# Block products in another order: the second sum last in its pair, the fourth third in the next pair, and the small projection's input loaded one pair earlier

## The reference

```python
y = (...) @ w_out                                    # 512 x 2048 by 2048 x 2048
x = _layernorm(DEEPNORM_ALPHA * x + y, post_ln_g[i], post_ln_b[i])
x = x + (p[i] @ ple_w[i]) * jax.nn.sigmoid(x @ ple_gate_w[i])
```

## Time and profile before

| what | value |
|---|---|
| median of 3 runs | 2092.15 us (2092.03 to 2092.24) |
| profiled execution, its own time | 2093.16 us |
| its span, first to last instruction | 2091.5 us |
| PE busy | 2081.2 us, 100% of the span |
| DVE busy | 1341.1 us, 64% |
| ACT busy | 873.3 us, 42% |
| POOL busy | 394.8 us, 19% |
| folded and last pairs of layer 0, layer 1 | about 861 to 986 us, 1758 to 1883 us |

### The profile page before, as it was taken

One profiled execution on the slowest core, in us unless ns is written; L12 is line 12 of the kernel. 1 busy time (PEld: TensorE's weight loads), 2 busy tenths in 40 slices (PEclk: granted clock), 3 DMA queues, 4 the chain that ended last, 5 costly groups with the idle time before them and its releaser, 6 DMA issues.

```text
span 2091.5 us, 29899 instructions
## 1 busy us (share of the span) xinstructions
PE 2081.2 (100%) x11050; PEld 1750.7 (84%) x11050; DVE 1341.1 (64%) x2295; ACT 873.3 (42%) x1148; POOL 394.8 (19%) x232
## 2 busy tenths in 40 slices
PE   9999999999999999999999999999999999999999
PEld 7878888888888888898788888888888888997888
DVE  5235575665765747787733588888888986887332
ACT  4225464464564657354622322222223453447221
POOL 0000000000000004110400034444857521104000
PEclk9999999999999999999999999999999999999999
DMA  8322222212222122684333322222222235852431
GB/s 320 141 101 88 75 80 80 78 63 81 71 90 80 60 80 81 167 221 145 106 109 121 136 100 85 96 101 101 98 87 98 101 121 128 214 159 81 144 110 69
DMA packets 46947, 233.51 MB, mean 112 GB/s; under 512 B 5456, under 2 KB 5728, under 8 KB 26896
## 3 DMA queue, kind: packets, MB, share of 16 engines
q1 hardware_dynamic: 35424, 190.33, 26.4%
q0 software_dynamic: 10000, 36.36, 7.0%
q10 hardware_dynamic: 1440, 5.77, 0.8%
HBM read 224.05 MB, written 8.39 MB: 111 GB/s over the span
## 4 chain that ended last, share of the span: by engine, by line
PE 97%; DMA 1%; ACT 1%; DVE 1%; issue 0%; ACTq 0%
PE G L745 84%; PE X L745 8%; PE T L745 5%; DMA w_raw<-wall_in 1%; PE T L927 1%; PE T L1048 0%; ACT w_hi L1484 0%; DVE w_lo L2194 0%; ACT a_hi L1235 0%; ACT Z L1430 0%; ACT Y L1577 0%; PE T L1053 0%; PE T L899 0%; DVE Y L2222 0%; ACT L1322 0%
## 5 line engine op out<-in xcount | busy, mean ns | idle before, releaser
L745 PE MATMUL G<-a_hi,w_hi 128*128 128x512 f32 (+1 forms) x2524 | 979.9, 388 | 3.3 <-DVE w_lo L2194 2.8
L745 PE MATMUL G<-a_hi,w_lo 128*128 128x512 f32 (+1 forms) x2524 | 974.0, 386 | 0.0
L745 PE MATMUL G<-a_lo,w_hi 128*128 128x512 f32 (+1 forms) x2524 | 972.2, 386 | 0.0
L1231 ACT ACTIVATE w_hi<-w_raw 128x2048 fp32r<-128x2048 f32 x147 | 281.7, 1916 | 788.0 <-PE G L745 775.2
L1705 DVE TENSOR_TENSOR w_lo<-w_raw,w_hi 128x2048 fp32r<-128x2048 f32 x104 | 242.1, 2328 | 494.7 <-ACT w_hi L1231 494.7
L745 PEld LDWEIGHTS G<-a_hi,w_hi 128*128 128x128 f32 x2524 | 474.2, 188 | 101.2 <-issue 4.0
L745 PEld LDWEIGHTS G<-a_hi,w_lo 128*128 128x128 f32 x2524 | 474.2, 188 | 95.7 <-issue 0.2
L745 PEld LDWEIGHTS G<-a_lo,w_hi 128*128 128x128 f32 x2524 | 474.3, 188 | 95.0 <-issue 0.5
L2429 DVE SCALAR_TENSOR_TENSOR T<-tmp,par,T 128x512 f32<-128x512 f32 x464 | 306.9, 749 | 0.0
L687 POOL TENSOR_TENSOR w_lo<-w_raw,w_hi 128x2048 fp32r<-128x2048 f32 x45 | 207.8, 4617 | 232.4 <-ACT w_hi L1231 232.4
L1484 ACT ACTIVATE w_hi<-w_raw 128x768 fp32r<-128x768 f32 (+1 forms) x86 | 66.3, 784 | 90.5 <-PE G L745 30.4
(11 more groups left out here) (336 smaller groups left out, 2249.2 us busy)
## 6 DMA issues: line engine op xcount, KB each, us to landing
w_raw<-wall_in SPq DMA_DIRECT2D x150, 1024.0 KB, 4.8
w_raw<-wall_in SPq DMA_DIRECT2D x42, 384.0 KB, 4.9
w_raw<-wall_in SPq DMA_DIRECT2D x36, 256.0 KB, 5.0
w_raw<-wall_in POOLq DMA_DIRECT2D x24, 384.0 KB, 5.4
Y<-w_in POOLq DMA_DIRECT2D x2, 2048.0 KB, 15.5
x_residual<-Y POOLq DMA_DIRECT2D x16, 256.0 KB, 3.6
out<-Y POOLq DMA_DIRECT2D x15, 256.0 KB, 3.6
Z<-xT_in SPq DMA_DIRECT2D x6, 512.0 KB, 9.2
```

The costliest lines, as they stand in the source:

```text
L745: return pe.matmul(o, l, r, start=start, stop=stop)
L1231: f(w_hi[:, w.slot, :], w_raw[:, w.slot, :], ACT.Copy).then_inc(S("w_hi"), 1)
```

## The change

- In all folded pairs the product of t2 is the last of its pair, behind b22 and b21, and the product of t4 is made in the next pair, behind r1 and r2 (in pair 7 too). High parts, low parts and the ring follow that order. In pair 7 the slots of b12 and b22 change places.
- POOL's list stays, so the sum for t4 and the two sums for the next pair are issued when the low part of t2 is done, which is later in the pair now. SP's list stays too: b21 of pair 3 still waits for the low part of pair 2's t4, and b12 of pair 7 for that of pair 6's t4, which are now made in pairs 3 and 7.
- `empty_products` is cut in two: `empty_most` (four operations) right after the low part of t2, `empty_rest` (three operations, behind t2's product) after the low part of t4 in the next pair.
- DVE's queue in pairs 3 to 6 is now: r1, r2, t4 of the pair before, `empty_rest`, finish_two, b11, t1, finish_one, `full_add`, t3, `full_add`, the bank copy, (pair 4 of layer 0: the small projection's input), centres, (a square), b22, b21, a square, t2, `empty_most`, a square.
- ACT issues the transfer of a pair's residual at the end of the pair before.
- POOL issues the small projection's input at the end of pair 2's list, and ACT rounds it at the end of pair 3.

```diff
-FOLDED = ("r1", "r2", "b11", "t1", "t3", "t2", "b22", "b21", "t4")
-FIRST_FOLDED = ("r1", "t1", "r2", "b11", "t3", "t2", "b22", "b21", "t4")
+FOLDED = ("r1", "r2", "b11", "t1", "t3", "b22", "b21", "t2")
+FIRST_FOLDED = ("r1", "t1", "r2", "b11", "t3", "b22", "b21", "t2")
...
-UNFOLDED_SLOTS = {"b12": 3, "b22": 2}
+UNFOLDED_SLOTS = {"b12": 2, "b22": 3}
...
+SEQUENCE = pieces(FOLD_FROM)
+for pair in range(FOLD_FROM + 1, FOLD_TO + 1):
+    SEQUENCE += pieces(pair)[:2] + [(pair - 1, "t4")] + pieces(pair)[2:]
+N_PIECES = len(SEQUENCE)
...
@@ POOL, weight_sums @@
-                    if (layer, p) == (0, FOLD_FROM + 1):
+                    if (layer, p) == (0, FOLD_FROM):
...
@@ PE, folded_pair @@
                 if p > FOLD_FROM:
+                    last_product(layer, p - 1)
                     pe.wait_ge(*emptied(layer, p - 1, 6))
...
+                piece_products(layer, p, "b22", two[:, 0:HALF_T], *fold(3), False, True).then_inc(done, 1)
+                piece_products(layer, p, "b21", one[:, 0:HALF_T], *tokens(twos_at, 0), False, False).then_inc(done, 1)
                 pe.wait_ge(*emptied(layer, p, 1))
                 piece_products(layer, p, "t2", first, *fold(2), True, True).then_inc(done, 1)
-                piece_products(layer, p, "b22", two[:, 0:HALF_T], *fold(3), False, True).then_inc(done, 1)
-                piece_products(layer, p, "b21", one[:, 0:HALF_T], *tokens(twos_at, 0), False, False).then_inc(done, 1)
-                piece_products(layer, p, "t4", one[:, HALF_T:T], *tokens(twos_at, 1), False, True).then_inc(done, 1)
...
@@ ACT, pairs 3 to 6 @@
                     piece_high(p, "r1")
                     piece_high(p, "r2")
+                    piece_high(p - 1, "t4")
+                    piece_high(p, "b11")
                     act.wait_ge(*summed(layer, p, "t1"))
                     act.wait_ge(*low_made(layer, p - 1, "b21" if p == FOLD_FROM + 1 else "t4"))
                     f(later, chain, ACT.Copy).then_inc(S("base_copied"), 1)
-                    piece_high(p, "b11")
...
                     piece_high(p, "b21")
-                    for n in c[-2:]:
-                        out_square(n)
-                    piece_high(p, "t4")
+                    out_square(c[-2])
+                    piece_high(p, "t2")
+                    if p + 1 < FOLD_TO:
+                        load_residual(p + 1)
+                    out_square(c[-1])
+                    if (layer, p) == (0, FOLD_FROM + 1):
+                        act.wait_ge(S("p_landed"), 16)
+                        f(p_hi.rearrange("p k t -> p (k t)"), p_raw0, ACT.Copy).then_inc(S("p_hi"), 1)
...
@@ DVE, pairs 3 to 6 @@
-                    lows(p, "r1")
+                    lows(p, "r1", "r2")
+                    lows(p - 1, "t4")
+                    empty_rest(p - 1)
                     finish_two(p - 1)
-                    lows(p, "r2", "b11")
+                    residual_in(p)
+                    lows(p, "b11", "t1")
                     finish_one(p - 1)
                     full_add(2 * p - 2)
-                    lows(p, "t1")
+                    lows(p, "t3")
                     full_add(2 * p - 1)
-                    lows(p, "t3", "t2")
                     empty_first(p)
...
-                    lows(p, "b22")
-                    lows(p, "b21")
+                    lows(p, "b22", "b21")
                     square_sums(c[-2:-1])
-                    lows(p, "t4")
+                    lows(p, "t2")
+                    empty_most(p)
                     square_sums(c[-1:])
-                    residual_in(p)
-                    empty_products(p)
```

More of the change, by code:

```diff
@@ L92, with pieces @@
 N_FOLDS = FOLD_TO - FOLD_FROM
-N_PIECES = N_FOLDS * len(FOLDED) + len(UNFOLDED)
+def pieces(p):
+    own = UNFOLDED if p == FOLD_TO else FIRST_FOLDED if p == FOLD_FROM else FOLDED
+    return [(p, name) for name in own]
+SEQUENCE = pieces(FOLD_FROM)
+for pair in range(FOLD_FROM + 1, FOLD_TO + 1):
+    SEQUENCE += pieces(pair)[:2] + [(pair - 1, "t4")] + pieces(pair)[2:]
+N_PIECES = len(SEQUENCE)
 HALVES = (64, 32, 16, 8)
@@ L460, in ring_free @@
             if (p, name) == (FOLD_TO, "b12"):
+                return piece_done(layer, p - 1, "t4")
+            if (p, name) == (FOLD_TO, "b22"):
                 return piece_done(layer, p, "b11")
@@ L1110, in piece_products, with tokens, last_product @@
                 return last
+            def tokens(chunks, half):
+                at = slice(half * HALF_T, (half + 1) * HALF_T)
+                return [a_hi[:, c, at] for c in chunks], [a_lo[:, c, at] for c in chunks]
+            def last_product(layer, p):
+                one, twos_at = out_banks(p)[0], range(PLAIN_K + PAIR_K, KC)
+                piece_products(layer, p, "t4", one[:, HALF_T:T], *tokens(twos_at, 1), False, True).then_inc(S("piece_done"), 1)
             def folded_pair(layer, p):
@@ L1545, in second_part @@
                     piece_high(p, "b21")
[L1546 to L1550 removed]
+                    out_square(c[-2])
+                    piece_high(p, "t2")
+                    if p + 1 < FOLD_TO:
+                        load_residual(p + 1)
+                    out_square(c[-1])
+                    if (layer, p) == (0, FOLD_FROM + 1):
+                        act.wait_ge(S("p_landed"), 16)
+                        f(p_hi.rearrange("p k t -> p (k t)"), p_raw0, ACT.Copy).then_inc(S("p_hi"), 1)
+                piece_high(FOLD_TO, "r1")
+                piece_high(FOLD_TO, "r2")
+                piece_high(FOLD_TO - 1, "t4")
+                piece_high(FOLD_TO, "b11")
+                piece_high(FOLD_TO, "b21")
                 out_square(11)
@@ L2217, in empty_products, with empty_rest @@
                     tt(Y4[:, two, 1, :], Y4[:, two, 1, :], q7, ALU.subtract).then_inc(step, 1)
+                def empty_rest(p):
+                    one, two = 2 * p, 2 * p + 1
+                    q6, step = TB[0][:, 0:HALF_T], S("fold_emptied")
+                    dve.wait_ge(*emptied(layer, p, 5))
                     dve.wait_ge(*piece_done(layer, p, "t2"))
```

41 lines of the change are left out of this document (16 added, 25 removed).

## The result

The changed kernel takes 2098.88 us (median of 8 runs, 2097.72 to 2101.26) beside 2092.54 (2092.03 to 2094.32) for the kernel before on the same chip: ratio 1.0031, 95% interval 1.0022 to 1.0039. It is slower by 6.3 us, which is more than the 0.2% that a measurement of this kernel can tell. The profiled execution took 2099.08, 5.9 more than the profiled one before. In the code of after, the matmuls are L754, the low parts L2216, the high parts L1499, finish_one is L2263, the copy of the next pair's base L1508, and the copy of t1's sum L1551.

The account below looks back on a forecast made before the run. PE was taken to bound the kernel, busy 2081.2 of 2091.5 us, with at most 5.6 us of waits to win. Terms -2.6 + 1.0 + 3.5 = +1.9 us on the median 2092.15 gave 2094.0, range 2090.3 to 2098.0.

Parts of the forecast that it names:

- the start of finish_one in pairs 4 to 6: DVE, pairs 4 to 6: finish_one waits for t4's product and starts 0.20 to 0.25 us after PE's end.
- Pair 2: First folded pair: waits at t4 and r1 go, b21 still waits behind ACT's copy; gain 2.6 us (bounds -0.2 and 5.6).
- SP's load "at nothing": SP's load of pair 3's b21 waits for t4's low part, with r1, r2, b11 of pair 4 behind: no cost.
- its own 2.63: Pair 2, both layers: 2.63 us from the start of ACT's copy to b21's first matmul.
- b22 of pair 3, +1.0: Pair 3: b22 can start at S + 18.8, PE there at S + 18.5; +1.0 us (bounds 0 and 9.6).
- The other steps at nothing: Residual's earlier transfer, b12's load in the last pair, the small projection's input and its split on ACT: no cost.
- DVE's tail: Pairs 4 to 6: DVE work from finish_one to the end of b22's low part, 6.51 us against PE's 6.48.
- The forecast's gap: Before b22, pairs 4 to 6: 0.40 us lost each, 1.54 in layer 0's pair 4; sum +3.5 us (bounds 0, 5.0).
- A: POOL's queue becomes late: three sums back to back, t3's late, each b22 0.69 later in 8 pairs; 2099.5 us; chance 0.22.
- B: No relief: pair 3's b11 lands as before, +2.8 us on the forecast, 2096.8 us; chance 0.12.
- D: DVE's tail doesn't reach PE in pairs 4 to 6: -2.6 + 1.0, 2090.5 us; chance 0.09.
- C: Equal turns between DMA queues: relief is whole, pair 2 has no gap; -1.1 us, 2091.0 us; chance 0.07.

Follow-up runs that it names:

- the two orders: Each alone against the changed kernel: b21's high part ahead of ACT's copy, 2095.70 us; b22's low part ahead of small projection's input and centres on DVE, 2095.10 us.
- both orders: Changed kernel with b21's high part ahead of ACT's copy and b22's low part ahead of the centres on DVE: 2092.63 us, ratio 1.0002 to before.
- the best version: t4's move alone against the kernel before, transfers in their old places, pair 3's r1 low part ahead of the emptying: 2088.87 us, ratio 0.9985.

## Why the prediction was wrong

It said 2094.0, from 2090.3 to 2098.0, most likely no change; it is 2098.88, and slower. The losses after were put at 7.5 us and were 11.2: 0.8 less in pair 2, 1.8 more in pair 3, 2.7 more in pairs 4 to 6. Two steps failed, the one at nothing that makes pair 3's wait, and the start of finish_one in pairs 4 to 6.

**Pair 2: right in its mechanism, a little better than said.** The waits for t4's sum and at r1 went, and b21 waits behind the copy. ACT's timeline of after, the copies and the two uses of sums, beside the earlier trace rows:

```profile
874.23 0.85 ACT L1508 ACTIVATE chain<-w_raw 128x768 f32<-128x768 f32 x1 [7.09 <-DMA w_raw<-wall_in]
...
896.26 0.84 ACT L1508 ACTIVATE chain<-w_raw 128x768 f32<-128x768 f32 x1 [6.27 <-DMA w_raw<-wall_in]
...
905.85 1.58 ACT L1499 ACTIVATE w_hi<-w_raw 128x768 fp32r<-128x768 f32 x2 [4.25 <-DMA w_raw<-wall_in]
909.40 0.85 ACT L1551 ACTIVATE w_raw<-chain 128x768 f32<-128x768 f32 x1 [1.96 <-DMA chain<-wall_in]
...
1774.52 0.85 ACT L1508 ACTIVATE chain<-w_raw 128x768 f32<-128x768 f32 x1 [6.35 <-DMA w_raw<-wall_in]
...
1796.09 0.84 ACT L1508 ACTIVATE chain<-w_raw 128x768 f32<-128x768 f32 x1 [5.80 <-DMA w_raw<-wall_in]
...
1810.06 0.84 ACT L1551 ACTIVATE w_raw<-chain 128x768 f32<-128x768 f32 x1 [3.53 <-DMA chain<-wall_in]
```

From each copy to b21's first matmul it is 2.63 us, in all four places, as in the earlier trace rows. Against before, with the later start of the stretch taken off (0.45 and 4.56), b11 of pair 3 landed 0.97 earlier in layer 0 (forecast 1.18) and 2.53 in layer 1 (forecast 1.59). The gain was 5.8 - 2.2 = 3.6 where 2.6 was said.

**The first step that failed: SP's load "at nothing".** The prediction saw the queue (b21 of pair 3 waits for t4's low part, and r1, r2 and b11 of pair 4 stand behind it) and the time at which b11 is wanted, some 10 us after t4's low part. It set no time of issue and landing beside that. By its own 2.63, b21 of pair 3 (due at 898.89 - 1.36 = 897.53) needs the copy at 894.90, which is 10.0 after SP's first issue behind t4's low part (884.91): the 10 us were right. The chain of waits in after shows when b11 was asked for and came:

```profile
878.58 4.44 DMA w_raw<-wall_in
883.05 0.86 ACT w_hi L1499
...
887.10 0.97 DVE w_lo L2216
888.09 8.10 DMA w_raw<-wall_in
...
```

It was issued at 888.09, when the low part of pair 3's b11 was done, and landed 8.1 us later, 11.3 after SP's issue at 884.91. PE doesn't stand in this chain from 875 to 925. 6.8 us would have done. A term of 1.36 + 0.89 and its slow steps was missing. The one in its place (b22 of pair 3, +1.0) was not there: it came from a t4's sum of 5.78 us, and the sum took 4.4. In layer 0 of the run with SP's other order, r1 and r2 no longer wait for t4's low part, b11 is issued at about the same time (888.19), and its copy starts at 894.58, 1.7 sooner. So part of the 8.1 is due to the loads that this wait held back until just ahead of b11. What else lay there? The DMA queues from 884 to 896.3 us, in after and then in before:

```profile
q0 software_dynamic: 482, 1.42, 50.7%
q1 hardware_dynamic: 731, 1.74, 40.5%
```

```profile
q1 hardware_dynamic: 577, 1.31, 34.9%
q0 software_dynamic: 279, 0.78, 34.3%
q10 hardware_dynamic: 144, 0.79, 16.7%
```

The residual (q10) has left this stretch, as the change wants, but two sums and the small projection's input have entered it. The engines are busy for 91% of it, before for 86%. Moving the input back alone changed nothing, and moving the residual back made the copy 2.2 later. How much of the 8.1 is each neighbour's stays open. The other steps at nothing held: no piece of the last pair starts late, nor does the small input's rounding stop PE.

**The second step that failed, in pairs 4 to 6: when finish_one starts.** DVE's tail behind it was sized right. The forecast's gap, 0.30 and in layer 0's pair 4 1.14 more, assumes that finish_one starts 0.20 after t4's end. DVE's timeline of after, pair 4 of layer 0:

```profile
911.01 0.96 DVE L2216 TENSOR_TENSOR w_lo<-chain,w_hi 128x768 fp32r<-128x768 f32 x1
911.88 0.68 DVE L2263 TENSOR_TENSOR Y<-Y,G 128x512 f32<-128x512 f32 x1
```

b11 began at 911.08, so finish_one should have stood at 911.28; it starts at 911.88. Two sums made it late. t4's came at 905.85, and from t4's low part on DVE has no pause up to b11's low part at 909.91; behind that, t1's low part (0.88) and the step to finish_one (0.86) would have given 911.65, 0.37 late. t1's sum added the other 0.23. The lateness of finish_one (its start less b11's start less 0.20) explains each gap:

| b22 of | finish_one late | late sum | gap due: 0.30 + that (+ 1.14) | gap measured |
|---|---|---|---|---|
| pair 4, layer 0 | 0.60 | t4's 0.37, t1's 0.23 | 2.04 | 2.01 |
| pair 5, layer 0 | 0.23 | t4's | 0.53 | 0.81 |
| pair 6, layer 0 | 0 | none | 0.30 | 0.26 |
| pair 4, layer 1 | 1.44 | t1's | 1.74 | 1.70 |
| pair 5, layer 1 | 0 | none | 0.30 | 0.27 |
| pair 6, layer 1 | 0.30 | t4's | 0.60 | 0.55 |

(In pair 5 of layer 0 DVE also idles 0.22 before t3's low part.) In pair 5 of layer 0 and in pair 6 of layer 1 DVE doesn't idle before t1's low part; it idles before t4's, and all behind that is as much later. Pair 5 of layer 0, DVE's timeline, then ACT's:

```profile
929.26 0.96 DVE L2216 TENSOR_TENSOR w_lo<-w_raw,w_hi 128x768 fp32r<-128x768 f32 x1 [3.90 <-ACT w_hi L1499]
```

```profile
928.38 1.58 ACT L1499 ACTIVATE w_hi<-w_raw 128x768 fp32r<-128x768 f32 x2 [5.68 <-DMA w_raw<-wall_in]
```

So DVE's tail was sized to a few hundredths, and the 2.7 us beyond the forecast's 3.5 come from late sums: 1.7 from t1's in two places, 0.9 from t4's in three. The prediction followed the landing of t4's sum only into pair 3, and its sum had nothing for t1's.

**The rivals.** A comes nearest in time (2099.5), and half of its mechanism is real: sums issued in a row after t2 come late. But the late ones are t1's and t4's, not t3's; together they cost 2.6 us in four places, not 0.69 in each of eight, and t3's low part kept DVE idle once only, for 0.22. B fell (b11 of pair 3 came earlier), D fell (b22 was late in every pair). C fell too. Its rule was that of the Trainium skill, DMA: Bandwidth & Descriptors, section Queues, rings and completion order: a DMA engine takes turns between the queues that have work. The shares of 50.7% and 40.5% above are near to equal turns. Those of the earlier trace rows are not, and POOL's queue was not short of work there: t4's sum was under way from 867.97 for 10.07 us, and beside its 16.8% SP's queue had 79.4%, in layer 1 73.6% beside 21.2%. So no run bears out equal shares as a rule. Nor did POOL's share bound the relief, which in layer 1 was 2.53 against the 1.59 of POOL's time.

**In sum.** t2 last takes the cover of b21 away and makes three sums begin late; undoing it alone gives 6.3 us back. About half of that shows through ACT's copy and half through DVE's tail (3.2 and 3.8 by the two orders). t4's move doesn't need t2's, and is worth 3.4 us with r1's low part brought forward, if the transfers stay where they were; as the change made it, with the early transfers, it was worth nothing (2092.63).

**Still open.** Why landings scatter. For the same code, b21 of pair 2 lost 1.49 in layer 0 and 0.75 in layer 1, and in the run with SP's order 1.8 in both. The 3.6 us between the median with both orders and 2089 are open too. Which neighbour held which transfer can't be settled from single profiles.

## What to carry to other kernels

A step that is set at nothing because "it is asked for early enough" needs two times beside each other, when it is wanted and when its transfer lands under the load that the change itself puts there; here that was 8.1 us for 384 KB, where 6.8 would have done. Try the parts of a change alone: here t4's move gained 3.4 us once its transfers were put back, and t2's move lost 6.3. Moving a load within a stretch where the DMA engines are 90% busy moves the late landing, and by layer 1's profiles its price changed sign with the order of the pieces around it. Follow every late transfer through the in-order queues behind it: in pair 5 of layer 0 a t4's sum that landed late, at 928.38, showed only at b22, at 941.04. And look at the granted clock behind a long wait of PE.

## What the hardware did that was not expected

**The third sum waits for the first to land.** POOL issues t4's, t1's and t3's sums in this order, and nothing in the program holds the third once its base has landed. POOL's timeline of after, pair 4:

```profile
900.77 0.86 POOL L638 DMA_DIRECT2D w_raw<-wall_in  x1 [13.20 <-DVE w_lo L2216]
901.31 1.21 POOL L635 DMA_DIRECT2D chain<-wall_in  x1
906.09 0.88 POOL L635 DMA_DIRECT2D other<-wall_in  x1 [3.57 <-issue]
```

The third goes out at 906.09, 0.24 after t4's sum had landed (905.85); in the other three pairs of layer 0 it is 0.33, 0.34 and 0.34. Before it was the same, t4's landing at 897.52 and then:

```profile
897.76 0.89 POOL L626 DMA_DIRECT2D other<-wall_in  x1 [3.16 <-issue]
```

Two adding transfers of this size under way seem to be as many as POOL puts out; a plain one of 512 KB followed the third after 0.56 (883.94). No run varied this, so the limit is read from the rows, not shown.

**The same bytes took from 4.4 to 9.3 us.** A sum's 384 KB took 4.4 us (878.58 to 883.05 in after), 5.1 (900.77 to 905.85), 8.1 (901.31 to 909.40, issued second) and 9.3 (behind the 512 KB, in the run of t4's move alone). An estimate by the Trainium skill, DMA: Bandwidth & Descriptors, section Anatomy of one DMA (2.0 us and the bytes at 436 GB/s for a transfer issued by GpSimd) would be 2.9; none of these came near it. None was alone; how long one takes alone wasn't tried.

**The kernel's scatter depends on the order.** The kernel with b22's low part first ran from 2092.16 to 2100.25 and the best version from 2087.84 to 2089.58. But b22's low part first on top of the best version had one run of 2098.06 among twelve. The longest runs of several kernels had a mean granted clock below full: 2100.25, 2106.79 and 2098.06 with 0.998, 2110.78 with 0.997, where most other runs had 0.999 or 1.0. Their waits weren't profiled; the profile with a clock of 0.50 behind a wait of 3.20 us shows one way in which a late landing costs more than its own wait.
